# Norm statistics of a two-block kernel computed in four column groups, and the factor spread by a product

## The chip, the cores and the metric

The kernel runs on one core of one Trainium2 chip. The metric is device microseconds of one execution, from launch to the end of the program; the profile adds a trace of one execution, with the engines PE (TensorE), DVE (VectorE), ACT (ScalarE), POOL and the DMA queues.

## The reference

Two blocks in float32 over 1024 tokens of width 1024. The first is a SwiGLU layer, a mixer of latent attention and a state-space scan, a second SwiGLU layer and a gated embedding, with a layer norm (ln1 to ln4) after each. The second begins with an RMS norm (here called "h") and a modulation, and mixes by gates, convolutions and a recurrence. What the change touches are the five norms:

```
def layer_norm(x, g, b):
    mu = jnp.mean(xf, axis=-1, keepdims=True)
    var = jnp.mean(jnp.square(xf - mu), axis=-1, keepdims=True)
    y = (xf - mu) * lax.rsqrt(var + LN_EPS)
    return y * g + b

x = layer_norm(ALPHA * x + 0.5 * swiglu(x, ffn1_w1, ffn1_w3, ffn1_w2), ln1_g, ln1_b)
...                                        # mixer, then ln2
x = layer_norm(ALPHA * x + 0.5 * swiglu(x, ffn2_w1, ffn2_w3, ffn2_w2), ln3_g, ln3_b)
ple = jax.nn.sigmoid(x @ ple_w_gate) * (p @ ple_w_proj)
x = layer_norm(ALPHA * x + ple, ln4_g, ln4_b)
h = x * lax.rsqrt(jnp.mean(x * x, axis=-1, keepdims=True) + RMS_EPS) * norm_g * (1 + scale) + shift
```

## The kernel before

**Layout.** The activations lie transposed: X is 128 partitions x 8 chunks x 1024 tokens, so the 1024 features are 8 chunks k of 128 partitions. Everything runs in two halves of 512 tokens (h = 0, 1), since one PSUM bank holds 128 x 512 float32. A product of full precision is made of three passes in the replicated format fp32r: both operands are kept as a high and a low part (XS[:, 0] and XS[:, 1] for X), and `group3` issues high-high, high-low and low-high. A product over 8 chunks is so 24 matmuls of 128x512 ("a product" below), one over 2 chunks 6, over 4 chunks 12.

**A norm** takes, for each half: the sum over chunks on DVE (HELD), a float32 product of all ones with it (bank "mean": every partition gets the sum), the subtraction on DVE (8 steps "c"), the squares on ACT (8 steps, into the free high half of XS, called XSf, or into SQ), their sum, the root on ACT, the reciprocal on DVE, 8 steps "y" (X times gain times factor) on DVE, each followed by a high part on ACT and a low part on DVE, both into XS. The sum of the squares goes over partitions by a float32 product with ones into the bank "var". For ln1 h0, ln3 h0, ln4 h1 and both halves of h it is accumulated on PE over the 8 chunks (`square_sum` and the loop in `norm`); for the five pairs in SUMMED DVE adds the chunks first, and one product is left. In all 45 such products. Since ones has 128 columns, every partition of the bank holds the same 512 sums, and the root and the reciprocal run on 128 x 512.

**Order.** Every engine has its own program, written out by hand; an engine goes through it in order and waits for events of the others (`ve(...)` for DVE, `ac(...)` for ACT, `mm(...)` for PE). The steps of a norm are a generator, `norm` or `merge_norm` (or `norm_h`, for ln4 and h together); `hook()` runs it on to its next `yield`, in the middle (k = 4) or at the end of a neighbouring product. So the norm of one half lies among products of the other half or of the next layer: ln1 h0 and ln3 h0 among the last down products of their own layer ("dn", 12 matmuls each, m = 0 to 7 of h1), ln1 h1 among the products of `latents`, ln2 h1 among the first up products of the second SwiGLU layer, ln3 h1 and ln4 h0 among those of `embed` (for every n a product "pg" of 24 matmuls and a product "pp" of 6, whose sum "pe" is made on DVE), ln4 h1 and h among the first products of the mixer.

**Banks.** PSUM banks are dealt out in turn by `banks`, a ring of 7 in the first SwiGLU layer and of 8 after it. `banks.take(use, end)` names the event that ends a use; whoever comes to the same bank one round later waits for it before his first matmul. TMP, five buffers of 512 columns, is dealt out in the same way by `tmps`.

Of the kernel before, what the change touches and what calls it, by code (L numbers as in the profile page):

```python
# [252 lines left out]
def build(nc, t, plan):  # L253
# [104 lines left out]
    GW = at("GW", 188.0625, [128, 3, 128], F32)  # L358
    HX = at("HX", 184, [128, 2, 512], F32)
    VA = at("VA", 56, [128, 1030], F32)  # L360
# [118 lines left out]
    def var_bank(name, h):  # L479

        return bank(name, "var", h) if name in LNS else bank("sq", name, h)

    def out_part(p):

        return slice(0, 512) if p == 0 else slice(256 + 256 * p, 512 + 256 * p)
# [79 lines left out]
    def tensor(e):  # L565
# [23 lines left out]
        def product8(u, h, use, tag, pair=xs_pair, beside=False, within=False):  # L589
            if h == 1 and not beside:  # L590
                flush()
            e.wait_ge(w_hi(u), w_lo(u), *banks.free(use))
            for k in range(8):
                if within and k == 4:
# [12 lines left out]
        def square_sum(name, h, n, src, width=512):  # L607
# [3 lines left out]
            for k in range(n):  # L611
                e.wait_ge(ac("sq", name, h, k))
                mms([(bank(*use)[:, 0:width], ones[:], src(k), k == 0, k == n - 1)]).then_inc(*mm.inc("sq", name, h, k))

        def norm(name, h):
            mean, var = (name, "mean", h), (name, "var", h)
            banks.take(mean, (ve, name, "mean", h))
            e.wait_ge(ve("ones"), ve(name, "sum", 7, h), *banks.free(mean))
            mms([(bank(*mean), ones[:], HELD[:, h, :], True, True)]).then_inc(*mm.inc(*mean))
            banks.take(var, (ac, "rs", name, h))  # L620
            yield
            if (name, h) in SUMMED:
                yield
                e.wait_ge(ve(name, "sqs", 7, h), *banks.free(var))
                mms([(bank(*var), ones[:], squares(name, 0, h), True, True)]).then_inc(*mm.inc(name, "var", 7, h))
            else:
                e.wait_ge(*banks.free(var))
                for k in range(8):
                    if k == 4:
                        yield  # L630
                    e.wait_ge(ac(name, "sq", k, h))
                    mms([(bank(*var), ones[:], squares(name, k, h), k == 0, k == 7)]).then_inc(*mm.inc(name, "var", k, h))
            yield
            yield
            yield

        def merge_norm(h):

            mean, var = ("ln2", "mean", h), ("ln2", "var", h)
            banks.take(mean, (ve, "ln2", "mean", h))  # L640
            e.wait_ge(ve("ones"), ve("ln2", "sum", 7, h), *banks.free(mean))
            mms([(bank(*mean), ones[:], HELD[:, h, :], True, True)]).then_inc(*mm.inc(*mean))
            yield
            banks.take(var, (ac, "rs", "ln2", h))
            e.wait_ge(ve("ln2", "sqs", 7, h), *banks.free(var))
            mms([(bank(*var), ones[:], squares("ln2", 0, h), True, True)]).then_inc(*mm.inc("ln2", "var", 7, h))
            yield
# [20 lines left out]
        def ffn(name, tag, with_mod):  # L668
# [4 lines left out]
            def up(fis):  # L673

                us = {fi: (w.take(), w.take()) for fi in fis}
                for h in range(2):
                    for fi in fis:
                        use1, use3 = (name, "up1", fi, h), (name, "up3", fi, h)
                        banks.take(use1, (ac, name, "silu", fi, h))
                        banks.take(use3, (ve, name, "mul", fi, h))  # L680
                        product8(us[fi][0], h, use1, tag, within=h == 0)
# [87 lines left out]
        def latents():  # L769
            us = {i: w.take() for i in (1, 2, 0, 3, 4, 5)}  # L770
            for n, (i, h) in enumerate(LATENTS):
# [5 lines left out]
                for k in range(8):  # L777
                    if k == 4 and n in (1, 2, 3):
                        hook()
# [319 lines left out]
        def merge():  # L1099
            nonlocal side  # L1100

            def out_product(u, m, h):
                use = ("wo", m, h)
                banks.take(use, (ve, *use))
                product8(u, h, use, "mh", pair=mh_pair, beside=h == 1, within=m in (3, 6) and h == 1 or None)
            us = [w.take() for _ in range(8)]
# [10 lines left out]
        def norm_h(h):  # L1117

            steps = norm("ln4", h)
            for _ in range(3):  # L1120
                next(steps)
                yield
            square_sum("h", h, 8, lambda k: SQ[k][:])
            yield

        def embed():
# [3 lines left out]
            for n, (m, h) in enumerate(EMBED):  # L1130
# [6 lines left out]
                banks.take(use, (ac, *use))  # L1137
                product8(us[m], h, use, "ln3", beside=True, within=n in (1, 2, 3, 8, 9, 10, 12) or None)
                if h == 1 or m < 4:
# [26 lines left out]
        def first_planes():  # L1166
# [4 lines left out]
            for h in range(2):  # L1171
                if h:
                    banks.skip()
                for i, (u, (name, sig, end)) in enumerate(zip(us, names)):
# [3 lines left out]
                    for k in range(8):  # L1178
                        if k == 4 and h == 0 and i < 2:
                            next(steps)  # L1180
# [160 lines left out]
    def scalar(e):  # L1341
# [46 lines left out]
        def root(name, h, n, eps, var, end=None, width=512):  # L1388

            use = ("rs", name, h)  # L1390
            tmps.take(use, (ve, *(end or use)))
            e.wait_ge(var, ve("eps"), *tmps.free(use))
            act(tmp(*use)[:, 0:width], var_bank(name, h)[:, 0:width], ACT.Sqrt, bias=EPS[eps], scale=1.0 / n).then_inc(*ac.inc(*use))

        def norm(name, h, dead, to_xs=True):
# [7 lines left out]
            yield  # L1403
            root(name, h, 1024, LN_EPS, mm(name, "var", 7, h))
            yield
# [509 lines left out]
        def embed():  # L1915
# [50 lines left out]
            biased(0)  # L1966
            root("h", 0, 1024, RMS_EPS, mm("sq", "h", 0, 7))
            gate(12)
# [39 lines left out]
        def mixer():  # L2008
            for ct in range(4):
# [46 lines left out]
                else:  # L2056
# [7 lines left out]
                    biased(1)  # L2064
                    root("h", 1, 1024, RMS_EPS, mm("sq", "h", 1, 7))
                    for k in range(8):
# [156 lines left out]
    def vector(e):  # L2223
# [64 lines left out]
        def rstd(name, h, out, width=512):  # L2288
            e.wait_ge(ac("rs", name, h))
            d.reciprocal(out[:, 0:width], tmp("rs", name, h)[:, 0:width]).then_inc(*ve.inc("rs", name, h))  # L2290

        def norm_add(name, i, h, src, ready, held, order=range(8)):

# [8 lines left out]
        def norm(name, h, src, ready, to_xs=True):  # L2302
# [13 lines left out]
            yield  # L2316
            e.wait_ge(ve(name, "c", 7, h))
            rstd(name, h, s)
            yield
# [824 lines left out]
        def h_rows(h):  # L3144
# [5 lines left out]

            rstd("h", h, HX[:, h, :])
            for k in range(8):
                e.wait_ge(ve("gc", 1), ve("rs", "h", h), ac("ln4", "y", k, h), *tmps.free(("hp", h, k)))
                stt(tmp("hp", h, k), X[:, k, half(h)], GC[:, 0, k:k + 1], HX[:, h, :], ALU.mult, ALU.mult).then_inc(
                    *ve.inc("hy", k, h))
# [947 lines left out]
```

## Time and profile before

| what | us |
|---|---|
| median of 3 runs | 3131.28 |
| lowest and highest | 3130.58, 3132.92 |
| the profiled execution | 3131.53 |
| its span in the trace | 3129.7 |
| PE busy | 3082.8 (98%) |
| DVE busy | 2368.0 (76%) |
| ACT busy | 1222.6 (39%) |

The span runs from the first to the last instruction in the trace; 1.8 us of the execution's time lie around it. Busy time counts instructions of the engine itself. A float32 matmul stands in the trace as two records, one for each half of its weights' bits, and its PEld records (weight loads) likewise.

### The profile page before, as it was taken

Reading aid. Unit: us, or ns where it says so; the run is one execution under the profiler, and the core shown is the slowest. Engines: PE = TensorE matmul, PEld = TensorE weight load, DVE = VectorE, ACT = ScalarE, POOL = GpSimd, SP = SyncE. Lnnn points to the kernel's source line nnn. Section 1 sums busy time; section 2 is a strip of 40 time slices with the busy share of each in tenths; the row PEclk is TensorE's granted clock in tenths of the full one; section 3 lists DMA queues with packets and bytes.
Section 4 is the critical chain, followed back from the end, with each engine's and each line's share of the span. In section 5 each row is a group of like instructions: output and inputs, shape, how many; then the busy total and the mean of one; then the engine's idle time right before and its main releaser. Section 6 shows DMA issues by size and latency. Waiting matters only on the chain.

```text
span 3129.7 us, 37552 instructions
## 1 busy us (share of the span) xinstructions
PE 3082.8 (98%) x14712; PEld 2490.4 (80%) x14712; DVE 2368.0 (76%) x4017; ACT 1222.6 (39%) x1884; POOL 56.2 (2%) x49
## 2 busy tenths in 40 slices
PE   8999999999999999999999999999999999999998
PEld 6887888877988887777878888888777788788887
DVE  6777767778869678888598776767797789789736
ACT  4233323335342455554243233222366534534414
POOL 0000000000000001130000000000000000000000
PEclk9999999999999999999999999999999999999999
DMA  3222212223343351012212111111211221122242
GB/s 131 74 73 75 81 61 68 68 68 109 119 101 135 115 197 56 8 48 114 95 54 68 41 54 61 48 54 48 68 54 63 104 77 64 48 70 101 81 168 74
DMA packets 89247, 250.13 MB, mean 80 GB/s; under 512 B 8560, under 2 KB 24816, under 8 KB 87536
## 3 DMA queue, kind: packets, MB, share of 16 engines
q1 hardware_dynamic: 89072, 247.73, 23.5%
q8 instruction: 118, 1.93, 0.3%
q14 instruction: 57, 0.47, 0.0%
HBM read 203.65 MB, written 44.04 MB: 79 GB/s over the span
## 4 chain that ended last, share of the span: by engine, by line
PE 90%; DVE 7%; ACT 2%; issue 1%; DMA 0%; DVEq 0%; SPq 0%; ACTq 0%
PE PS L577 88%; PE PS L582 2%; DVE WS L2228 1%; DVE X L2236 1%; DVE XS L2236 1%; DVE HELD L2290 1%; DVE X L2228 1%; ACT XS L1345 0%; DVE COLB L3038 0%; DVE XSf L2228 0%; ACT XSf L1345 0%; DVE TMP L2228 0%; DMA RAW<-in_W 0%; DVE TMP L2232 0%; ACT WS L1345 0%
## 5 line engine op out<-in xcount | busy, mean ns | idle before, releaser
L577 PE MATMUL PS<-XS,WS 128*128 128x512 f32 (+1 forms) x6480 | 1513.8, 391 | 20.4 <-DVE XS L2228 9.5
L577 PEld LDWEIGHTS PS<-XS,WS 128*128 128x128 f32 x6480 | 1208.9, 188 | 297.8 <-issue 27.1
L577 PE MATMUL PS<-HS,WS 128*128 128x512 f32 x2208 | 511.0, 390 | 3.1 <-DVE TMP L2228 2.7
L577 PEld LDWEIGHTS PS<-HS,WS 128*128 128x128 f32 x2208 | 414.1, 188 | 93.1 <-DVE TMP L2228 3.5
L2228 DVE TENSOR_TENSOR WS<-RAW,WS 128x512 fp32r<-128x512 f32 (+1 forms) x398 | 346.9, 880 | 173.8 <-ACT WS L1345 173.2
L1345 ACT ACTIVATE WS<-RAW 128x512 fp32r<-128x512 f32 (+1 forms) x398 | 307.6, 779 | 398.7 <-PE PS L577 344.0
L2228 DVE TENSOR_TENSOR X<-PS,X 128x512 f32<-128x512 f32 x272 | 184.2, 688 | 101.8 <-PE PS L577 101.7
L2228 DVE TENSOR_TENSOR TMP<-TMP,PS 128x512 f32<-128x512 f32 x304 | 203.6, 682 | 61.5 <-PE PS L577 58.7
L577 PE MATMUL PS<-T,WS 128*128 128x512 f32 x960 | 230.6, 389 | 0.0
L577 PEld LDWEIGHTS PS<-T,WS 128*128 128x128 f32 x960 | 180.2, 188 | 37.4
L1345 ACT ACTIVATE TMP<-PS 128x512 f32<-128x512 f32 x144 | 85.0, 596 | 291.0 <-PE PS L577 274.4
L2236 DVE SCALAR_TENSOR_TENSOR CV<-UU,COL,CV 128x1024 f32<-128x1024 f32 x120 | 154.0, 1283 | 3.4
L1345 ACT ACTIVATE HS<-TMP 128x512 fp32r<-128x512 f32 x88 | 55.6, 632 | 211.3 <-DVE TMP L2236 197.2
L577 PE MATMUL PS<-T1h_ln,WS 128*128 128x512 f32 x320 | 105.0, 389 | 0.0
L577 PE MATMUL PS<-KH,QH 128*128 128x512 f32 x384 | 104.0, 406 | 0.0
L1345 ACT ACTIVATE TMP<-TMP 128x512 f32<-128x512 f32 x80 | 50.6, 632 | 101.3 <-DVE TMP L2228 101.3
L2228 DVE TENSOR_TENSOR HS<-TMP,HS 128x512 fp32r<-128x512 f32 x88 | 60.6, 689 | 32.3 <-ACT HS L1345 32.1
L3038 DVE TENSOR_REDUCE COLB<-PS 128x1 f32<-128x1024 f32 x64 | 77.9, 1218 | 5.7 <-PE PS L577 4.6
L577 PE MATMUL PS<-MH,WS 128*128 128x512 f32 x256 | 80.3, 393 | 0.0
L1345 ACT ACT_TABLE_LOAD x56 | 71.8, 1283 | 15.1 <-DVE GG L2228 10.7
L1345 ACT ACTIVATE WS<-RAWX 128x512 fp32r<-128x512 f32 x66 | 41.4, 627 | 91.2 <-PE PS L577 91.1
L577 PEld LDWEIGHTS PS<-KH,QH 128*128 128x128 f32 x384 | 67.5, 189 | 11.3
(338 smaller groups left out, 3580.6 us busy)
## 6 DMA issues: line engine op xcount, KB each, us to landing
RAW<-in_W SPq DMA_DIRECT2D x263, 512.0 KB, 3.3
RAWX<-in_W SPq DMA_DIRECT2D x30, 512.0 KB, 3.3
DC<-TMP SPq DMA_DIRECT2D x32, 256.0 KB, 2.1
X<-in_xT SPq DMA_DIRECT2D x8, 512.0 KB, 8.9
DX<-X SPq DMA_DIRECT2D x2, 2048.0 KB, 8.4
DCZ<-CA SPq DMA_DIRECT2D x8, 512.0 KB, 4.1
DGA<-TMP SPq DMA_DIRECT2D x16, 256.0 KB, 2.3
DGB<-TMP SPq DMA_DIRECT2D x16, 256.0 KB, 3.1
```

The lines of the kernel that those rows point to most:

```text
L577: done = d.matmul(out, l, r, start=first, stop=last)
L582: done = d.transpose(out, x, idn)
L1345: return d.activation(out, x, f, bias=bias, scale=scale)
L2228: return d.tensor_tensor(out, a, b, op)
L2236: return d.scalar_tensor_tensor(out=out, in0=a, scalar=s, in1=b, op0=op0, op1=op1)
L2290: d.reciprocal(out[:, 0:width], tmp("rs", name, h)[:, 0:width]).then_inc(*ve.inc("rs", name, h))
L3038: d.tensor_reduce(mx, PS[:, 2 + 2 * (n % 2):4 + 2 * (n % 2), :], AX.XY, ALU.max).then_inc(*ve.inc("mx", n))
```

## The change

Five things change, and the SUMMED list and all other sums of squares (kv, q, cx, c, out) stay.

1. **Sum of squares.** `quarter_sums` replaces each of the 45 products by four, each with 32 columns of ones and 128 tokens: quarter g of the half goes to partitions 32g to 32g+31 of the bank, columns 0 to 127.
2. **Root and reciprocal** run on 128 x 128; the reciprocal is written in place, into TMP, and HX is dropped.
3. **`spread`** is new: four float32 products of 128x128, whose weights are column 32g of the identity, repeated 128 times. They put row 32g of the reciprocal on all partitions, into columns 128g to 128g+127 of the same bank. It waits for the reciprocal. It happens ten times, once for each norm and half.
4. **The steps y** (and "hy", for h) take the factor from that PSUM bank instead of HELD or HX, and wait for the spread.
5. **The bank "var"** (and "sq" for h) is freed by the last of the eight steps y, before by the root. Extra hooks at k = 7 give the spread its place, 9 matmuls after the sum where both are in one product.

```
+        def quarter_sums(out, src, first, last):
+            return mms([(out[32 * g:32 * g + 32, 0:128], ones[:, 0:32], src[:, 128 * g:128 * g + 128], first, last)
+                        for g in range(4)])
+        def spread(name, h):
+            r = tmp("rs", name, h)
+            e.wait_ge(ve("rs", name, h), dma("const")("cols"))
+            mms([(var_bank(name, h)[:, 128 * g:128 * g + 128], ident[:, 32 * g:32 * g + 1].to_broadcast([128, 128]), r[:, 0:128], True, True)
+                 for g in range(4)]).then_inc(*mm.inc("rb", name, h))
...
         def norm(name, h):
-            banks.take(var, (ac, "rs", name, h))
+            banks.take(var, (ve, name, last_scaled(name), 7, h))
             yield
             if (name, h) in SUMMED:
                 yield
                 e.wait_ge(ve(name, "sqs", 7, h), *banks.free(var))
-                mms([(bank(*var), ones[:], squares(name, 0, h), True, True)]).then_inc(*mm.inc(name, "var", 7, h))
+                quarter_sums(bank(*var), squares(name, 0, h), True, True).then_inc(*mm.inc(name, "var", 7, h))
...
-            yield
-            yield
+            yield
+            spread(name, h)
             yield
...
-                product8(us[m], h, use, "ln3", beside=True, within=n in (1, 2, 3, 8, 9, 10, 12) or None)
+                product8(us[m], h, use, "ln3", beside=True,
+                         within={1: (4,), 2: (4,), 3: (4, 7), 8: (4,), 9: (4,), 10: (4, 7), 12: (4, 7)}.get(n))
...
+        def rstd_rows(name, h):
+            r = tmp("rs", name, h)[:, 0:128]
+            e.wait_ge(ac("rs", name, h))
+            d.reciprocal(r, r).then_inc(*ve.inc("rs", name, h))
...
-                e.wait_ge(ve("rs", name, h), ac(name, "sq", 7, h))
-                scaled = stt(x, x, col(name + "_g", k), s, ALU.mult, ALU.mult)
+                e.wait_ge(mm("rb", name, h), ac(name, "sq", 7, h), ve(name, "c", 7, h))
+                scaled = stt(x, x, col(name + "_g", k), var_bank(name, h), ALU.mult, ALU.mult)
```

PE around the sum of squares of ln3 h1, in `embed`, before. XSf holds the squares, XS the activations of the products pg, HS (with WS) those of the products pp; the x23 and x5 rows end a product each:

```order
2729 L577 MATMUL PS<-XSf,ones 128x512 [waits vector_done]
2730 L577 MATMUL PS<-XS,WS 128x512 x12
2731 L577 MATMUL PS<-HS,WS 128x512 [waits vector_done]
2732 L577 MATMUL PS<-HS,WS 128x512 x5
2733 L577 MATMUL PS<-XS,WS 128x512 [waits activation_done,weight_lo_done,weight_hi_done]
2734 L577 MATMUL PS<-XS,WS 128x512 x23
2735 L577 MATMUL PS<-HS,WS 128x512 [waits weight_lo_done,weight_hi_done]
2736 L577 MATMUL PS<-HS,WS 128x512 x5
2737 L577 MATMUL PS<-XS,WS 128x512 [waits activation_done]
```

The same place after. TMP holds the reciprocal:

```order
2767 L579 MATMUL PS<-XSf,ones 32x128 [waits vector_done]
2768 L579 MATMUL PS<-XSf,ones 32x128 x3
2769 L579 MATMUL PS<-XS,WS 128x512 x9
2770 L579 MATMUL PS<-TMP,ident 128x128 [waits vector_done]
2771 L579 MATMUL PS<-TMP,ident 128x128 x3
2772 L579 MATMUL PS<-XS,WS 128x512 x3
2773 L579 MATMUL PS<-HS,WS 128x512 x6
2774 L579 MATMUL PS<-XS,WS 128x512 [waits activation_done,weight_lo_done,weight_hi_done]
2775 L579 MATMUL PS<-XS,WS 128x512 x23
2776 L579 MATMUL PS<-HS,WS 128x512 [waits weight_lo_done,weight_hi_done]
2777 L579 MATMUL PS<-HS,WS 128x512 x5
2778 L579 MATMUL PS<-XS,WS 128x512 [waits vector_done]
```

Row 2770, the spread, is new and waits for the reciprocal. Row 2778 is the first matmul of pg(5, 0), which comes to the bank of the sum one round of 8 later: before it waited for ACT's root (row 2737), now for DVE's last step y.

PE at the last down products of the first SwiGLU layer (ln1 h0), from the second run of sums on, before; the last product is dn m = 7, which comes to the bank of the sum in a ring of 7:

```order
797 L577 MATMUL PS<-XSf,ones 128x512 [waits activation_done] x4
798 L577 MATMUL PS<-HS,WS 128x512 x24
799 L577 MATMUL PS<-HS,WS 128x512 [waits vector_done]
800 L577 MATMUL PS<-HS,WS 128x512 x11
801 L577 MATMUL PS<-HS,WS 128x512 [waits vector_done]
802 L577 MATMUL PS<-HS,WS 128x512 x11
803 L577 MATMUL PS<-HS,WS 128x512 [waits activation_done]
804 L577 MATMUL PS<-HS,WS 128x512 x11
```

Rows 798 to 804 are dn m = 3 to 7. The same place on PE after, from the last sum on:

```order
810 L579 MATMUL PS<-XSf,ones 32x128 [waits activation_done]
811 L579 MATMUL PS<-XSf,ones 32x128 x3
812 L579 MATMUL PS<-HS,WS 128x512 x12
813 L579 MATMUL PS<-TMP,ident 128x128 [waits vector_done]
814 L579 MATMUL PS<-TMP,ident 128x128 x3
815 L579 MATMUL PS<-HS,WS 128x512 x36
816 L579 MATMUL PS<-HS,WS 128x512 [waits vector_done]
817 L579 MATMUL PS<-HS,WS 128x512 x11
```

The spread stands after m = 3 (row 813), and m = 7 (row 816) waits for the last step y of ln1 h0. On DVE and ACT no instruction changes its place; root, reciprocal and the eight steps y stand where they stood.

## Rows read from the trace of the kernel before

**Rows 1.** The page, busy time of each engine.

```profile
PE 3082.8 (98%) x14712; PEld 2490.4 (80%) x14712; DVE 2368.0 (76%) x4017; ACT 1222.6 (39%) x1884; POOL 56.2 (2%) x49
```

**Rows 2.** PE by time, eight sums of squares of h h0: start, us, count.

```profile
2360.96 7.03 PE L577 MATMUL PS<-SQ,ones 128*128 128x512 f32 x16
2367.42 3.30 PE L577 MATMUL PS<-XS,WS 128*128 128x512 f32 x12
2370.56 1.52 PE L577 MATMUL PS<-HS,WS 128*128 128x512 f32 x6
```

**Rows 3.** PE by time, products in two column groups of 64, then full ones.

```profile
906.83 1.97 PE L577 MATMUL PS<-UB,BW 128*64 128x128 f32 x32
908.73 1.09 PE L582 MATMUL PS<-ident,BT 128*128 128x128 f32 x8
909.75 1.97 PE L577 MATMUL PS<-UB,BW 128*64 128x128 f32 x32
```

**Rows 4.** Groups by form, DVE: count, busy us, mean ns.

```profile
L2290 DVE RECIPROCAL HELD<-TMP 128x512 f32<-128x512 f32 x11 | 36.9, 3350 | 17.1 <-ACT TMP L1345 17.1
L2290 DVE RECIPROCAL HELD<-TMP 128x256 f32<-128x256 f32 x3 | 5.2, 1750 | 1.2 <-ACT TMP L1345 1.2
L2236 DVE SCALAR_TENSOR_TENSOR X<-PS,MOD,X 128x512 f32<-128x512 f32 x40 | 29.7, 747 | 46.6 <-PE PS L577 41.4 <-DMA X<-DX 5.2
```

**Rows 5.** By time, ln1 h0: DVE around its reciprocal, PE at its end.

```profile
699.91 3.35 DVE L2290 RECIPROCAL HELD<-TMP 128x512 f32<-128x512 f32 x1 [1.93 <-ACT TMP L1345]
704.45 1.41 DVE L2236 SCALAR_TENSOR_TENSOR X<-X,COL,HELD 128x512 f32<-128x512 f32 x2
716.47 0.75 DVE L2236 SCALAR_TENSOR_TENSOR X<-X,COL,HELD 128x512 f32<-128x512 f32 x1
...
712.60 3.71 PE L577 MATMUL PS<-XS,WS 128*128 128x512 f32 x15
```

**Rows 6.** By time, ln3 h1: PE, then DVE, then ACT.

```profile
2295.62 1.02 PE L577 MATMUL PS<-XSf,ones 128*128 128x512 f32 x2
2306.05 1.52 PE L577 MATMUL PS<-HS,WS 128*128 128x512 f32 x6
2307.41 5.60 PE L577 MATMUL PS<-XS,WS 128*128 128x512 f32 x24
2331.95 1.02 PE L577 MATMUL PS<-HELD,ones 128*128 128x512 f32 x2
...
2300.79 3.34 DVE L2290 RECIPROCAL HELD<-TMP 128x512 f32<-128x512 f32 x1
2305.13 1.40 DVE L2236 SCALAR_TENSOR_TENSOR X<-X,COL,HELD 128x512 f32<-128x512 f32 x2
2319.96 0.75 DVE L2236 SCALAR_TENSOR_TENSOR X<-X,COL,HELD 128x512 f32<-128x512 f32 x1
...
2300.86 1.06 ACT L1345 ACTIVATE WS<-RAW 128x1024 fp32r<-128x1024 f32 x1 [3.50 <-PE PS L577]
```

**Rows 7.** By time, ln4 and h of h0: DVE, then ACT.

```profile
2349.57 3.34 DVE L2290 RECIPROCAL HELD<-TMP 128x512 f32<-128x512 f32 x1
...
2367.34 1.28 ACT L1345 ACT_TABLE_LOAD   x1
```

**Rows 8.** By time, ln4 and h of h1: PE, then DVE.

```profile
2410.58 11.46 PE L577 MATMUL PS<-XS,WS 128*128 128x512 f32 x48
...
2443.45 23.60 PE L577 MATMUL PS<-XS,WS 128*128 128x512 f32 x102 [0.40 <-ACT XS L1345]
...
2429.67 3.35 DVE L2290 RECIPROCAL HX<-TMP 128x512 f32<-128x512 f32 x1 [8.92 <-ACT TMP L1345]
```

**Rows 9.** Three stretches: us; PE, PEld, DVE, ACT, POOL busy; granted clock.

```profile
712.00:753.00 41.00, 36.16 (x145) 26.20 (x144) 36.09 (x50) 22.11 (x35) 0.00 (x0) 0.99 0.33 117
749.00:752.40 3.40, 1.73 (x7) 0.84 (x6) 3.27 (x6) 2.11 (x3) 0.00 (x0) 1.00 0.31 115
752.40:755.80 3.40, 3.40 (x8) 2.49 (x9) 2.99 (x9) 2.24 (x4) 0.00 (x0) 0.50 0.00 0
```

More of the change, by code:

```diff
@@ L358, in build @@
     GW = at("GW", 188.0625, [128, 3, 128], F32)
-    HX = at("HX", 184, [128, 2, 512], F32)
     VA = at("VA", 56, [128, 1030], F32)
@@ L481, in var_bank, with last_scaled @@
         return bank(name, "var", h) if name in LNS else bank("sq", name, h)
+    def last_scaled(name):
+        return "y0" if name == "ln4" else "y"
     def out_part(p):
@@ L593, in product8 @@
             for k in range(8):
-                if within and k == 4:
+                if within and k in within:
                     hook()
@@ L631, in norm @@
                     e.wait_ge(ac(name, "sq", k, h))
-                    mms([(bank(*var), ones[:], squares(name, k, h), k == 0, k == 7)]).then_inc(*mm.inc(name, "var", k, h))
+                    quarter_sums(bank(*var), squares(name, k, h), k == 0, k == 7).then_inc(*mm.inc(name, "var", k, h))
             yield
-            yield
+            spread(name, h)
             yield
@@ L643, in merge_norm @@
             yield
-            banks.take(var, (ac, "rs", "ln2", h))
+            banks.take(var, (ve, "ln2", "y", 7, h))
             e.wait_ge(ve("ln2", "sqs", 7, h), *banks.free(var))
-            mms([(bank(*var), ones[:], squares("ln2", 0, h), True, True)]).then_inc(*mm.inc("ln2", "var", 7, h))
+            quarter_sums(bank(*var), squares("ln2", 0, h), True, True).then_inc(*mm.inc("ln2", "var", 7, h))
+            yield
+            spread("ln2", h)
             yield
@@ L680, in up @@
                         banks.take(use3, (ve, name, "mul", fi, h))
-                        product8(us[fi][0], h, use1, tag, within=h == 0)
+                        product8(us[fi][0], h, use1, tag, within=None if h else (4, 7) if fi else (4,))
                         product8(us[fi][1], h, use3, tag, within=None if h == 0 else False)
@@ L777, in latents @@
                 for k in range(8):
-                    if k == 4 and n in (1, 2, 3):
+                    if k == 4 and n in (1, 2, 3) or k == 7 and n == 3:
                         hook()
@@ L1104, in out_product @@
                 banks.take(use, (ve, *use))
-                product8(u, h, use, "mh", pair=mh_pair, beside=h == 1, within=m in (3, 6) and h == 1 or None)
+                product8(u, h, use, "mh", pair=mh_pair, beside=h == 1, within={3: (4,), 6: (4, 7)}.get(m) if h else None)
             us = [w.take() for _ in range(8)]
@@ L1119, in norm_h @@
             steps = norm("ln4", h)
-            for _ in range(3):
+            for _ in range(4):
                 next(steps)
                 yield
-            square_sum("h", h, 8, lambda k: SQ[k][:])
+            use = ("sq", "h", h)
+            banks.take(use, (ve, "hy", 7, h))
+            e.wait_ge(*banks.free(use))
+            for k in range(8):
+                e.wait_ge(ac("sq", "h", h, k))
+                quarter_sums(bank(*use), SQ[k], k == 0, k == 7).then_inc(*mm.inc("sq", "h", h, k))
+            yield
+            spread("h", h)
             yield
@@ L1178, in first_planes @@
                     for k in range(8):
-                        if k == 4 and h == 0 and i < 2:
+                        if k == 4 and h == 0 and i in (0, 1, 2, 4):
                             next(steps)
@@ L1390, in root @@
             use = ("rs", name, h)
-            tmps.take(use, (ve, *(end or use)))
+            tmps.take(use, (mm, "rb", name, h) if width == 128 else (ve, *(end or use)))
             e.wait_ge(var, ve("eps"), *tmps.free(use))
@@ L1403, in norm @@
             yield
-            root(name, h, 1024, LN_EPS, mm(name, "var", 7, h))
+            root(name, h, 1024, LN_EPS, mm(name, "var", 7, h), width=128)
             yield
@@ L1966, in embed @@
             biased(0)
-            root("h", 0, 1024, RMS_EPS, mm("sq", "h", 0, 7))
+            root("h", 0, 1024, RMS_EPS, mm("sq", "h", 0, 7), width=128)
             gate(12)
@@ L2064, in mixer @@
                     biased(1)
-                    root("h", 1, 1024, RMS_EPS, mm("sq", "h", 1, 7))
+                    root("h", 1, 1024, RMS_EPS, mm("sq", "h", 1, 7), width=128)
                     for k in range(8):
@@ L2316, in norm @@
             yield
-            e.wait_ge(ve(name, "c", 7, h))
-            rstd(name, h, s)
+            rstd_rows(name, h)
             yield
@@ L3149, in part @@
                     ALU.add, ALU.subtract).then_inc(*ve.inc("xs", "h", k, h))
-            rstd("h", h, HX[:, h, :])
+            rstd_rows("h", h)
             for k in range(8):
-                e.wait_ge(ve("gc", 1), ve("rs", "h", h), ac("ln4", "y", k, h), *tmps.free(("hp", h, k)))
-                stt(tmp("hp", h, k), X[:, k, half(h)], GC[:, 0, k:k + 1], HX[:, h, :], ALU.mult, ALU.mult).then_inc(
+                e.wait_ge(ve("gc", 1), mm("rb", "h", h), ac("ln4", "y", k, h), *tmps.free(("hp", h, k)))
+                stt(tmp("hp", h, k), X[:, k, half(h)], GC[:, 0, k:k + 1], var_bank("h", h), ALU.mult, ALU.mult).then_inc(
                     *ve.inc("hy", k, h))
```

## The prediction, made before the changed kernel ran

> **What bounds the kernel now.** The page comes first: PE is busy for 3082.8 of 3129.7 us [rows 1]. Where PE is never idle, a change is worth what it takes from PE's own work. So the next view is PE by time around each norm, with DVE and ACT beside it: which of them is late when PE comes to a product that needs the norm. The last are the groups by form, for the price of one instruction.
>
> A product of 128x512 costs 0.227 us in a row (2306.05 to 2307.41 for six) [rows 6]. Eight float32 sums of squares cost 2370.56 - 2360.96 - 12 x 0.227 = 6.88 us, 0.86 each [rows 2]; the busy time of such a row overlaps its neighbour's, so I go by starts.
>
> **The sums in column groups.** The nearest case is UB,BW, whose products write 64 of the 128 columns. Let p be one record over 128 tokens, s the cost of a change of shape. The full ones: 8p + s = 909.75 - 908.73 = 1.02. The halves: 32 records in 908.73 - 906.83 = 1.90, and if two run side by side 16p + s = 1.90 [rows 3]. That gives p = 0.11 and s = 0.14, and 0.11 is what 128 tokens in a two-record product should take if 512 take 0.43. Two groups do run side by side. No row shows four. Bounds: four side by side, 2p = 0.22 a product; pairs only, 0.44; nothing side by side, 0.88, as much as now. I take 0.22, since the step from one group to two cost nothing, and two changes of shape (0.28) for every run. The 45 products are six runs of four, two of eight and five single ones: 38.7 us before, 9.9 + 13 x 0.28 = 13.5 after. A single one costs 0.5, a run of four 1.2, one of eight 2.0.
>
> The row shows loads of the second group going on beside the first group's products. The Trainium skill says otherwise ("TensorE: Matmul & The Clock Gate", Part 3, The mechanism): weight loads overlap with running products only where the row group differs, and these share it. By that rule four groups run one after the other, and the sums cost 4.5 us more than now; by the row they cost 25 us less.
>
> **The spread** is eight full records, 8p = 0.88 to 1.02 with a change [rows 3]; I take 0.95, ten times 9.5. **On PE alone** the change is 13.5 + 9.5 - 38.7 = -15.7 us.
>
> **DVE.** A reciprocal takes 3350 ns on 512 columns and 1750 on 256 [rows 4], 6.25 ns a column; on 128 some 950 (bounds 150 and 1750, the line is the nearest). That is 2.4 us less, ten times. The steps y read the factor from PSUM; a step with a PSUM source takes 747 ns [rows 4], one from SBUF 0.75 us [rows 5]: nothing. The root gets shorter too; no term rests on it.
>
> **Where it lies.** What counts is the path, and two waits are new on PE, which works in order: the spread waits for the reciprocal, and the bank of the sum is held until the eighth step y, so that whoever comes one round later waits for that.
>
> *ln1.* DVE is free at 697.98 (699.91 less 1.93) [rows 5]; the sums end by then, and the reciprocal runs to 698.95, PE spreads until 699.9, and y begins at 700.1 against 704.45. All behind it on DVE moves by 4.35, and the last y (716.47 + 0.75) ends at 712.87. dn m = 7, in a ring of seven, can't begin before; PE would be there at 708.0 (699.9 and 36 products): a wait of 4.9 us. It ends at 715.6, 3.0 later than before (712.60). Then XS is all there, and the stretch 712 to 753, with 4.8 us idle on PE [rows 9], takes 4.1 less: 3.2 for waits on XS that fall away, 0.9 for h1, whose shorter root lets ACT go on to XS earlier. Sum -1.1.
>
> *ln2.* Single sums: 0.36 saved, 0.95 for the spread, and at h1 1.3 of waiting for a reciprocal, which shorter waits on XS give back: +0.6 and -0.2, together +0.4.
>
> *ln3 h0* repeats ln1 h0 with a ring of eight; the wait moves to the first product of `embed`, which waited for XS anyway: -0.2, bounds -1 and +2.
>
> *ln3 h1* is the largest term. The sum starts at 2295.6, nine products on, at 2298.2, PE comes to the spread. The reciprocal starts at 2300.79 without having waited for anything but DVE's queue [rows 6], ends at 2301.7: PE waits 3.6. Spread to 2302.7, nine products to 2304.7. ACT's copy of a weight at 2300.86 had waited 3.50 for that same end of pp(3, 0) [rows 6], and now goes at 2304.9; with its 1.06 and DVE's low half (1.0, the time between reciprocal and first y) y starts at 2307.1, 2.0 later than 2305.13 although the reciprocal was shorter. The last y ended 15.6 after the first: now 2322.7. PE has done 30 more products by 2311.5 and stands before pg(5, 0) for 11.2 us. It starts 15.3 later than 2307.41; up to the mean at 2331.95 there are 24.5 us with 102 products (23.1), so 1.4 of slack comes back: +13.9. If DVE moved 2.4 earlier instead of 2.0 later, it would be +9.5; with ACT's copy later by another 2, +16.
>
> *ln4 and h, h0.* The reciprocal at 2349.57 hangs on DVE's queue [rows 7] and ends at 2350.5; PE is there 1.5 earlier. The eight sums of h then take 2.0 instead of 6.9, but ACT loads its table for the root at 2367.34 without a wait [rows 7]: its queue sets it, not the sums, and shifts by 1.1 with PE's lateness. Root and reciprocal end at 2371.1, PE waits 4.0, and is through with pg(0, 1) at 2372.7 against 2370.56: +2.1.
>
> *ln4 and h, h1* gains. Two runs save 4.6: 2411.0 becomes 2406.4. 12 products, spread, 36 products, eight sums, 12 products and spread give 2424.1; the factor before was there at 2429.67 + 3.37 = 2433.0 [rows 8]. PE waits for XS up to 2443.45 [rows 8], so all 8.9 count: -8.9.
>
> Sum: -1.1 + 0.4 - 0.2 + 13.9 + 2.1 - 8.9 = +6.2.
>
> **The clock.** From 749.0 to 752.4 PE was busy for 1.73 of 3.40 us, and in the next 3.4 us the granted clock was 0.50 (1.2 GHz instead of 2.4) and PE did 8 products where 15 fit [rows 9]: 1.6 us. In four of the new waits (4.9, 3.6, 11.2, 4.0) PE idles longer than the 1.7 us of that stretch. I count three falls: +4.8, bounds 0 and 10. Span 3129.7 + 6.2 + 4.8 = 3140.7; with the 1.8 us around it 3142.5, and the median of the runs lies 0.25 under the profiled execution: 3142.
>
> **Rivals.** (1) *The clock stays up*, as over the lighter idling of rows 8: 3137.5. (2) *Groups don't run side by side*, a product's weights waiting for the product before: 0.88 each. The runs of ln4 and h in h1 cost 10.4 more, ln1 h0 and ln3 h0 some 1.6 each as the sum becomes late for DVE, single ones 0.6: 3158; pairs only, 3147. The skill's rule would give the first. (3) *Faster:* the wait of pg(5, 0) for its bank is the one place that decides. If the last y of ln3 h1 comes before PE gets there, at 2311.5, the 13.9 shrink to the 2.4 of the spread's wait, and with one fall of the clock less the time is 3129; below 3125 if the other spreads find their reciprocal ready. That needs 8.6 us from the reciprocal to the last y where the trace has 19.9 [rows 6], with two weights and the sum pe of pp(3, 0) between. Against it also: before, the bank was needed 13.3 us ahead of that y.
>
> **Numbers.** Forecast with two to five falls 0.62 (3139 to 3148); rival 1 0.14; pairs only 0.08; none side by side 0.04; faster or near it 0.12. Range 3133 to 3151. A measurement can tell 0.2% (6.3 us) from no change. Slower by more takes the forecast, both cases of (2) and half of (1): 0.81; within, half of (1) and half of (3): 0.13; faster 0.06.
>
> **What would show it.** XSf and SQ sums at 32x128 with four starts a few ns apart and a run of four in 1.2 us; reciprocals near 0.95; PE idle about 11 us before pg(5, 0), 5 before dn m = 7, 4 before the spread of h h0, released by DVE; granted clock 0.5 after them; the stretch from h1's mean of ln4 to the mixer 9 us shorter; PE's own work 15 us less. It is wrong if PE doesn't idle at pg(5, 0), or if the sums take as long as now.

## The result, and the profile after

| what | before | after |
|---|---|---|
| median of 4 runs each, us | 3132.1 | 3146.97 |
| lowest and highest | 3130.58, 3132.93 | 3145.39, 3150.2 |
| the profiled execution's span | 3129.7 | 3146.6 |
| granted clock, mean over the span | 0.998 | 0.993 |

The changed kernel is slower by 0.49% (ratio 1.0049, 95% interval 1.0034 to 1.0065), 14.9 us by the medians and 16.9 us by the spans. The forecast was 3142 and its range 3133 to 3151.

The page of the changed kernel, busy time of each engine (it answers to [rows 1]), and from its list of groups the two kinds of products that wait most, with what ended most of their waiting:

```profile
PE 3075.7 (98%) x15062; PEld 2498.8 (79%) x15062; DVE 2345.7 (75%) x4017; ACT 1220.1 (39%) x1884; POOL 56.2 (2%) x49
...
L579 PE MATMUL PS<-XS,WS 128*128 128x512 f32 (+1 forms) x6480 | 1512.7, 391 | 28.1 <-DVE X L2260 13.2
...
L579 PE MATMUL PS<-HS,WS 128*128 128x512 f32 x2208 | 516.2, 393 | 7.8 <-DVE X L2260 4.6
```

PE, DVE and ACT all have less to do than before. But PE waits, and 13.2 + 4.6 us of that are ended by one line of DVE, L2260, the helper that issues the steps y among others. So the view to open next is PE by time where those waits lie. The largest is at ln3 h1 (it answers to [rows 6]):

```profile
2296.57 0.43 PE L579 MATMUL PS<-XSf,ones 128*32 128x128 f32 x8
2296.93 2.34 PE L579 MATMUL PS<-XS,WS 128*128 128x512 f32 x9
2302.66 2.08 PE L579 MATMUL PS<-TMP,ident 128*128 128x128 f32 x8 [3.39 <-DVE TMP L2320]
2304.39 1.63 PE L579 MATMUL PS<-XS,WS 128*128 128x512 f32 x3
2305.81 2.75 PE L579 MATMUL PS<-HS,WS 128*128 128x512 f32 x6
2308.37 5.67 PE L579 MATMUL PS<-XS,WS 128*128 128x512 f32 x24
2313.88 1.52 PE L579 MATMUL PS<-HS,WS 128*128 128x512 f32 x6
2326.50 8.43 PE L579 MATMUL PS<-XS,WS 128*128 128x512 f32 x24 [11.09 <-DVE X L2260]
```

The sum is four side-by-side quarters, 0.36 us from its start to the next product's. Nine products on, PE waits 3.39 us for the reciprocal, and the spread takes twice what it takes elsewhere. Then pg(5, 0) waits 11.09 us for the bank. DVE and ACT in the same stretch show why it is 11:

```profile
2301.66 0.94 DVE L2320 RECIPROCAL TMP<-TMP 128x128 f32<-128x128 f32 x1
2309.75 1.23 DVE L2252 TENSOR_TENSOR WS<-RAW,WS 128x1024 fp32r<-128x1024 f32 x1 [7.15 <-ACT WS L1369]
2310.89 1.40 DVE L2260 SCALAR_TENSOR_TENSOR X<-X,COL,PS 128x512 f32<-128x512 f32 x2
...
2325.70 0.74 DVE L2260 SCALAR_TENSOR_TENSOR X<-X,COL,PS 128x512 f32<-128x512 f32 x1
```

```profile
2308.66 1.06 ACT L1369 ACTIVATE WS<-RAW 128x1024 fp32r<-128x1024 f32 x1 [11.22 <-PE PS L579]
```

The reciprocal is done at 2302.6, and the first y starts at 2310.89, because DVE's low half of a weight stands before it, that waits for ACT's copy at 2308.66, and that for the end of PE's product pp(3, 0). The eighth y ends at 2326.44; pg(5, 0) starts at 2326.50.

The clock, in windows of the changed kernel (start and end, length, the busy times of PE, PEld, DVE, ACT and POOL with their counts, the granted clock, DMA share and GB/s):

```profile
2302.70:2308.40 5.70, 5.70 (x18) 4.83 (x19) 0.00 (x0) 0.00 (x0) 0.00 (x0) 0.50 0.00 0
...
2326.50:2332.30 5.80, 5.80 (x14) 4.54 (x15) 4.55 (x7) 1.19 (x2) 0.00 (x0) 0.50 0.00 0
...
2391.80:2397.20 5.40, 5.40 (x17) 4.63 (x18) 1.41 (x2) 2.27 (x4) 0.00 (x0) 0.50 0.00 0
```

After the waits of 3.4, 11.1 and 3.8 us PE worked for 5.4 to 5.8 us at 1.2 GHz, and after that of 4.6 us before dn m = 7 for 3.4 us. Before, there was one such stretch near a norm, of 3.4 us [rows 9].

The other places. dn m = 7 at the end of ln1 h0, which answers to [rows 5], and the eight sums and the spread of h h0, which answer to [rows 2]:

```profile
701.27 8.44 PE L579 MATMUL PS<-HS,WS 128*128 128x512 f32 x36
714.35 4.62 PE L579 MATMUL PS<-HS,WS 128*128 128x512 f32 x12 [4.64 <-DVE X L2260]
...
2383.76 1.95 PE L579 MATMUL PS<-SQ,ones 128*32 128x128 f32 x64
2385.65 2.33 PE L579 MATMUL PS<-XS,WS 128*128 128x512 f32 x9
2391.79 2.08 PE L579 MATMUL PS<-TMP,ident 128*128 128x128 f32 x8 [3.81 <-DVE TMP L2320]
```

And where the change gains, from the mean of ln4 h1 to the last wait for XS of h h1 (it answers to [rows 8]):

```profile
2420.52 1.02 PE L579 MATMUL PS<-HELD,ones 128*128 128x512 f32 x2
...
2443.95 1.96 PE L579 MATMUL PS<-SQ,ones 128*32 128x128 f32 x64
...
2460.14 0.93 PE L579 MATMUL PS<-XS,WS 128*128 128x512 f32 x3 [0.39 <-ACT XS L1369]
```

39.6 us; before, the mean started at 2395.04 and the last wait ended at 2443.45, 48.4 us.

**The ledger.** PE's instructions other than those of the norms are the same in both kernels, so the start of each can be compared. "Lateness" is how much later such an instruction starts in the changed kernel than in the one before, in us:

| stretch | lateness at its end | gained or lost in it | forecast, without the clock |
|---|---|---|---|
| start to ln1 | +1.5 | +1.5 | 0 |
| ln1 | +1.2 | -0.3 | -1.1 |
| ln2 and mixer | +0.9 | -0.2 | +0.4 |
| ln3 h0 | +1.0 | 0.0 | -0.2 |
| ln3 h1 | +20.5 | +19.5 | +13.9 |
| ln4 and h, h0 | +25.5 | +5.0 | +2.1 |
| ln4 and h, h1 | +16.7 | -8.8 | -8.9 |

One norm of ten makes more than the whole loss. What is left in dispute is why: the bank that is held, the new wait for the reciprocal, the clock, or the column groups.

### The profile page after: what moved, and what is told of

Its sections match the earlier page's. It is cut to its first block, busy times and chain, and to the rows that moved or that the text cites. A ratio compares the mean times of both kernels' runs of the same rounds, so it can differ in the third digit from the quotient of the medians.

```text
span 3146.6 us, 38237 instructions
## 1 busy us (share of the span) xinstructions
PE 3075.7 (98%) x15062; PEld 2498.8 (79%) x15062; DVE 2345.7 (75%) x4017; ACT 1220.1 (39%) x1884; POOL 56.2 (2%) x49
## 4 chain that ended last, share of the span: by engine, by line
PE 90%; DVE 7%; ACT 2%; issue 1%; DMA 0%; DVEq 0%; SPq 0%; ACTq 0%
PE PS L579 88%; PE PS L584 2%; DVE X L2252 1%; DVE WS L2252 1%; DVE X L2260 1%; DVE XS L2260 1%; ACT WS L1369 0%; ACT XSf L1369 0%; DVE COLB L3067 0%; DVE XSf L2252 0%; DVE TMP L2252 0%; ACT XS L1369 0%; ACT X L1369 0%; DVE HELD L2252 0%; DMA RAW<-in_W 0%
## 5 line engine op out<-in xcount | busy, mean ns | idle before, releaser
L579 PE MATMUL PS<-XS,WS 128*128 128x512 f32 (+1 forms) x6480 | 1512.7, 391 | 28.1 <-DVE X L2260 13.2
L2260 DVE SCALAR_TENSOR_TENSOR CV<-UU,COL,CV 128x1024 f32<-128x1024 f32 x120 | 154.1, 1284 | 3.4
L579 PEld LDWEIGHTS PS<-KH,QH 128*128 128x128 f32 x384 | 67.5, 189 | 11.2
```

The costliest lines, as they stand in the source:

```text
L579: done = d.matmul(out, l, r, start=first, stop=last)
L2260: return d.scalar_tensor_tensor(out=out, in0=a, scalar=s, in1=b, op0=op0, op1=op1)
```

## The experiments

The kernels below are made from the changed one by sets of norms, (name, h), at the top; without them they are instruction for instruction the changed kernel, or with an empty QUARTER the one before:

```
+QUARTER = all ten        # column groups, root and reciprocal on 128 columns, spread
+HOLD = QUARTER           # the bank of the sum is freed by the last step y
+COPY = SKIP = SWAP = LATER = none
+    def var_end(name, h):
+        if (name, h) in COPY:
+            return (ve, "fc", name, h)
+        if (name, h) in HOLD:
+            return (ve, "hy", 7, h) if name == "h" else (ve, name, last_scaled(name), 7, h)
+        return (ac, "rs", name, h)
...
-            banks.take(var, (ve, name, last_scaled(name), 7, h))
+            banks.take(var, var_end(name, h))
```

Each was timed in turns with the kernel before on the same chip; its median there was 3131.5 or 3131.6 us. The changed kernel itself was timed only with the result above (3146.97, where the kernel before had 3132.1), and its four runs lie 4.8 us apart, so a small difference to it says little.

### One bank left out: pg(5, 0)

```
+SKIP = {("ln3", 1)}
...
+                if n == 0 and ("ln3", 0) in SKIP or n == 5 and ("ln3", 1) in SKIP:
+                    banks.skip()
                 banks.take(use, (ac, *use))
```

> The changed kernel, but pg(5, 0) leaves out the bank that holds the factor of ln3 h1 and takes the next one of the ring (and all behind it move on by one). My theory is that the held bank causes the 11.1 us of idle before pg(5, 0) and the half clock after it. Then pg(5, 0) starts right after pp(4, 0), at about 2315.4 instead of 2326.5, at full clock (5.6 us for its 24 matmuls instead of 8.3); 1.5 us of slack that the late start had used come back as a wait. 3147 - 11.1 - 2.9 + 1.5 = 3134.5, bounds 3131 and 3138. The rival is that something else is late there (the squares, the activations of h1, a weight): the idle time then stays before pg(5, 0) or one product later, and the time stays above 3142.

Measured: 3133.9 us (ratio 1.0007, 0.9998 to 1.0016). PE by time at the same place:

```profile
2307.90 5.71 PE L591 MATMUL PS<-XS,WS 128*128 128x512 f32 x24
2313.45 1.52 PE L591 MATMUL PS<-HS,WS 128*128 128x512 f32 x6
2314.82 5.60 PE L591 MATMUL PS<-XS,WS 128*128 128x512 f32 x24
2320.26 1.52 PE L591 MATMUL PS<-HS,WS 128*128 128x512 f32 x6
```

pg(5, 0) now starts at 2314.82, right behind pp(4, 0), at full clock; nothing waits in its place. Another bank for this product gives back 13 of the 14.9 us. The half clock after the 3.4 us wait for the reciprocal is still there.

### The hold alone, on the kernel before

```
+QUARTER = none
+HOLD = all ten
```

> The kernel before with one thing of the change: the bank of the sum of squares of all ten norms is freed by the last step y and no longer by the root. Sums, root, reciprocal and steps y stay as they were; there is no spread. My theory is that holding the bank is what costs: in ln3 h1 the last y ended at 2320.7 where pg(5, 0) began at 2307.4, so +13.3, less 1.4 of slack, and 3 of half clock; in ln1 h0 the last y ended at 717.2 where PE comes to dn m = 7 at 709.9, so 7.3 and 2.7 of half clock, of which some 6 come back from the waits on XS; ln3 h0 +2. Together 3132 + 15 + 4 + 2 = 3153, bounds 3146 and 3159. The rival is that the spread and its waits are the cost and the hold is covered: then 3132 to 3135.

Measured: 3158.46 us (1.0084, 1.007 to 1.0097), 26.9 us slower, without a single one of the other edits. PE by time where it waits:

```profile
717.30 5.00 PE L591 MATMUL PS<-HS,WS 128*128 128x512 f32 x12 [7.23 <-DVE X L2282]
...
2281.55 2.04 PE L591 MATMUL PS<-XS,WS 128*128 128x512 f32 x4 [4.71 <-DVE X L2282]
...
2332.39 7.47 PE L591 MATMUL PS<-XS,WS 128*128 128x512 f32 x24 [13.20 <-DVE X L2282]
```

The waits of 7.2 and 13.2 us are those that were worked out; the one of pg(0, 0), 4.7, was taken as 2, and less of the first came back (lateness 9.5 after dn m = 7, still 6.5 at the end of ln1). That makes most of the 5 us over the estimate. The rival falls. The hold costs the old kernel more than a copy saves the changed one (20 us, below); its wait before dn m = 7 is 7.2 us against 4.6, since the changed kernel's shorter sums, root and reciprocal bring y forward there.

### The gain alone: ln4 h1 and h h1

```
+QUARTER = {("ln4", 1), ("h", 1)}
```

> The kernel before with the whole change, but for ln4 h1 and h h1 alone (24 of the 45 sums, two spreads). My theory is that the stretch from the mean of ln4 h1 to the mixer is where the change pays: it was 48.4 us before and 39.6 after, so 3132 - 8.8 = 3123, bounds 3121 and 3126. The rival is that this gain came from the late start of that stretch (DVE and ACT had 20 us more to run ahead of PE): then PE waits for XS as before and the time is 3128 to 3132.

Measured: 3123.52 us (0.9971, 0.996 to 0.9983). PE comes to this stretch within 1 us of the kernel before and is 8.05 us ahead behind it. The gain is the change's own and doesn't hang on the 25 us by which PE came late to it.

### The width of the column groups

```
-            return mms([(out[32 * g:32 * g + 32, 0:128], ones[:, 0:32], src[:, 128 * g:128 * g + 128], first, last)
+            return mms([(out[:, 0:128], ones[:], src[:, 128 * g:128 * g + 128], first and g == 0, last and g == 3)
                         for g in range(4)])
```

> The changed kernel, but the four products of a sum have all 128 columns of ones and the same target, so that they can't run side by side and each occupies the whole array (all four are added up into the same 128 columns, so the factor is not the right one; only the time counts). If the four column groups ran side by side in the changed kernel, a sum now takes 0.88 us instead of some 0.25: 45 x 0.63 = 28 us of PE work more, of which 10 lie in ln4 h1 and h h1, where nothing covers them, and about 7 more on the paths of the two h0 norms of the SwiGLU layers and the single sums; the rest goes into waits that are there anyway. 3147 + 18 = 3165, bounds 3158 and 3172. If the groups ran one after the other there too, nothing changes: 3147.

Measured: 3164.51 us (1.0105, 1.0091 to 1.0119). The run of four sums in ln4 h1, PE by time, here and then in the changed kernel (for each the sums and the product after them; the difference of the starts is the cost):

```profile
2431.48 3.73 PE L597 MATMUL PS<-SQ,ones 128*128 128x128 f32 x32
2434.97 2.98 PE L597 MATMUL PS<-XS,WS 128*128 128x512 f32 x12
```

```profile
2426.95 1.08 PE L579 MATMUL PS<-SQ,ones 128*32 128x128 f32 x32
2427.97 3.01 PE L579 MATMUL PS<-XS,WS 128*128 128x512 f32 x12
```

3.49 against 1.02 us for the same 32 records over the same tokens. At full width a sum costs 0.87 us, as much as one product of 128x512 had cost [rows 2]; in four column groups 0.25. The edit also gives the four products one target. That is not what costs: the four products of a spread, full width too, go to four ranges of columns, and their 8 records take 0.81 us (2434.77 to 2435.58), 0.10 each, where 3.49 us for 32 is 0.11.

The first 30 ns of the same two runs, instructions on SQ alone (length, then busy time and count of PE, PEld, DVE, ACT), first in the changed kernel and then at full width:

```profile
2426.95:2426.98 0.03, 0.03 (x4) 0.03 (x4) 0.00 (x0) 0.03 (x1) 1.00 0.00 0
```

```profile
2431.48:2431.51 0.03, 0.03 (x1) 0.03 (x1) 0.00 (x0) 0.03 (x1) 1.00 0.00 0
```

Four products and four weight loads against one of each. So the quarters do run side by side, and this is worth 17.5 us to the changed kernel. The Trainium skill's rule ("TensorE: Matmul & The Clock Gate", Part 3, The mechanism), that weight loads overlap with running products only where the row group differs, is not what this case shows: all four share their rows. That the groups would then run one after the other was the prediction's own inference from that rule, not a statement of the page.

### A copy of the factor

```
+COPY = QUARTER
...
+            if (name, h) in COPY:
+                e.wait_ge(mm("rb", name, h))
+                d.tensor_copy(kept, var_bank(name, h)).then_inc(*ve.inc("fc", name, h))
+                return kept, ve("fc", name, h)
```

`kept` is HELD, or HX for h, as in the kernel before.

> The changed kernel, but DVE copies the factor from its bank into SBUF right after the spread (one instruction of 128x512, 0.7 us, ten times) and frees the bank with that; the steps y read the copy. By the theory of the held banks the waits before dn m = 7, pg(0, 0) and pg(5, 0) go (with their half clock), as they did when those three left the bank out (3129.4), and the wait of 4.9 us at 1177 which came with the shifted ring doesn't come, with 2 of half clock. Against it stand 0.7 us later activations in ln1, ln3 h0, ln4 h1 and h h1, where PE waits for them: +3. 3129.4 - 5 + 3 = 3127.5, bounds 3124 and 3131. The rival is that DVE's ten copies push back more than they free: above 3134.

Measured: 3127.13 us (0.9982, 0.9973 to 0.9991), with four single runs from 3122.24 to 3122.83 and seven from 3127.07 to 3128.49. The trace is of the fastest, so its lateness (-9.3 us at the end) holds for the four. By form, DVE:

```profile
L2348 DVE COPY HELD<-PS 128x512 f32<-128x512 f32 x8 | 5.5, 690 | 6.7 <-PE PS L591 6.7
...
L2348 DVE COPY HX<-PS 128x512 f32<-128x512 f32 x2 | 1.4, 691 | 2.5 <-PE PS L591 2.5
```

Seven us of DVE work take away the waits for a bank before dn m = 7, pg(0, 0) and pg(5, 0): by the medians 20 us less than the changed kernel. With all ten norms changed it is 0.2% faster than the kernel before. The trace also prices the clock: at ln3 h1 PE waits as long for the reciprocal as in the changed kernel, but in this execution the clock stays up.

```profile
2293.17 1.16 PE L591 MATMUL PS<-TMP,ident 128*128 128x128 f32 x8 [3.41 <-DVE TMP L2342]
...
2296.23 5.60 PE L591 MATMUL PS<-XS,WS 128*128 128x512 f32 x24
```

Spread and nine products take 3.06 us from start to start, in the changed kernel 5.71 (2302.66 to 2308.37): 2.65 us for that fall alone.

### Three banks left out

```
+SKIP = {("ln1", 0), ("ln3", 0), ("ln3", 1)}
```

> The changed kernel, but dn m = 7 of the first SwiGLU layer, pg(0, 0) and pg(5, 0) each leave out the bank that holds a factor (ln1 h0, ln3 h0, ln3 h1) and take the next one. By the theory that the held banks cause all three waits: as for ln3 h1 alone, 3134.5, less what dn m = 7 gains. It starts 4.6 us earlier and at full clock, which brings the down products of h1, and with them the norm of ln1 h1, 5 us forward (bounds 0 and 6.5), and pg(0, 0) 1 (bounds 0 and 2): 3128.5, bounds 3125 and 3134. The rival for these two is that the activations XS come at the same time whichever bank is used: then the same time as for ln3 h1 alone.

Measured: 3129.35 us (0.9994, 0.9985 to 1.0002), 4.6 below the kernel with one bank left out: the activations didn't come at the same time regardless. PE is 5.8 us ahead of the kernel before at the end of ln1. It loses that later, in the mixer:

```profile
1181.99 2.47 PE L591 MATMUL PS<-CKV,WS 128*128 128x512 f32 x5 [4.88 <-DVE TMP L2274]
```

The kernel with the copies comes there 6 us ahead too and doesn't wait. Leaving a bank out moves all later uses on by one, so that every later use has another predecessor; that points to the ring, but was not tried alone.

### The spread of h h0 later

```
-                         within={1: (4,), 2: (4,), 3: (4, 7), 8: (4,), 9: (4,), 10: (4, 7), 12: (4, 7)}.get(n))
+                         within={1: (4,), 2: (4,), 3: (4, 7), 8: (4,), 9: (4,), 10: (4, 7), 12: (4,), 13: (7,)}.get(n))
```

> The changed kernel, but the spread of h h0 stands in the product after the next, 30 matmuls (6.8 us) later. Its wait of 3.8 us for the reciprocal, which hangs on ACT's queue, is then covered, and the 6.8 us of half clock behind it (3.4 us of work) don't come, if the clock fell because PE idled there: 3147 - 3.8 - 3.4 = 3140, bounds 3137 and 3142. If the clock falls whatever stands there, 3143.5. The rival is that the factor was needed then, so that the steps y 3 us later give a wait for XS or for the bank: 3147.

Measured: 3144.9 us (1.0044, 1.003 to 1.0057), between the forecast (bounds up to 3142) and the rival, so neither came. The 2.1 us to the changed kernel are less than the spread of its four runs; the traces give 2.2. PE by time, at the spread and at the mean of ln4 h1:

```profile
2394.04 1.05 PE L597 MATMUL PS<-TMP,ident 128*128 128x128 f32 x8
...
2416.76 2.07 PE L597 MATMUL PS<-HELD,ones 128*128 128x512 f32 x2 [3.26 <-DVE HELD L2284]
```

The spread waits for nothing and takes 1.05 us, not 2.08. Behind it PE is 7.2 us ahead of the changed kernel. It was 0.6 ahead before this place, so 6.6 are due to the edit: the 3.8 of the wait and 2.7 for the 5.4 us of work at half clock (forecast 3.8 and 3.4). Without the idle stretch the clock didn't fall here, in this one trace. Then 5.0 of the 7.2 go again. DVE goes through the steps y and the last sums for the mean of ln4 h1 at its own pace:

```profile
2416.01 0.69 DVE L2284 TENSOR_TENSOR HELD<-HELD,X 128x512 f32<-128x512 f32 x1
```

```profile
2418.07 0.69 DVE L2252 TENSOR_TENSOR TMP<-TMP,PS 128x512 f32<-128x512 f32 x1 [2.72 <-PE PS L579]
2418.79 0.69 DVE L2252 TENSOR_TENSOR X<-X,TMP 128x512 f32<-128x512 f32 x1
2419.52 0.69 DVE L2252 TENSOR_TENSOR HELD<-HELD,X 128x512 f32<-128x512 f32 x1
```

The first row is the last addition before the mean here, the last row that of the changed kernel. There DVE waited 2.72 us for PE; here PE, 7 us further, waits 3.26 for DVE, and with the wait the half clock comes back. The rival had the direction, that most of it returns as a wait, but the wait is for the sum of ln4 h1, which neither reading had named.

### Nine of ten norms

```
+QUARTER = all ten without ("ln3", 1)
```

> The changed kernel with one of its ten norms put back: ln3 h1 sums, takes root and reciprocal and frees its bank as in the kernel before. By the starts on PE this norm alone cost 19.6 us (lateness of 1.1 at the mean of ln3 h1, 20.6 at that of ln4 h0): 3147 - 19.6 = 3127.4, bounds 3124 and 3131, which is faster than the kernel before. The rival is that the lateness only gathers there, and DVE, ACT or the other held banks would bring half of it in later (ln4 h0, h h0): 3132 to 3140.

Measured: 3129.08 us (0.9992, 0.9983 to 1.0001; single runs from 3125.71 to 3130.28), 17.9 us less than the whole change, and no different from the kernel before. The lateness doesn't gather there, it arises there.

### The norms that pay

```
+QUARTER = {("ln1", 0), ("ln1", 1), ("ln3", 0), ("ln4", 1), ("h", 0), ("h", 1)}
+SKIP = {("ln3", 0)}
+SWAP = {("ln1", 0)}
+LATER = {("ln3", 0)}     # its spread one yield later
... within: 12: (4,), 13: (7,)
```

> The change for ln1 (both halves), ln3 h0, ln4 h1 and both halves of h; ln2, ln3 h1 and ln4 h0 as in the kernel before. dn m = 7 swaps its bank with its follower in the ring, pg(0, 0) leaves the held bank out, the spread of ln3 h0 stands one product of 12 later (it had waited 2.0) and that of h h0 30 matmuls later (it had waited 3.8). By my ledger of PE starts: ln1 -6.2, and no 4.9 us of idle at 1177 since the ring keeps its phase; ln3 h0 -2.5 to -4.5; h h0 -3.6 (eight sums 6.9 to 2.0, spread 0.95, changes of shape); ln4 h1 and h h1 -8.6. Together 3132 - 22 = 3110, bounds 3106 and 3119. The rival is that DVE and ACT set the time once PE is 10 us ahead of where it was, and the gains of ln1 and ln3 come back as waits: 3119 to 3123.

Measured: 3117.84 us (0.9957, 0.9945 to 0.997). That is inside the bounds, but 8 us over the estimate and close to the rival's 3119. PE by time, the two waits that took most of the difference:

```profile
713.75 2.55 PE L597 MATMUL PS<-XS,WS 128*128 128x512 f32 x10 [2.11 <-DVE X L2292]
...
2387.70 1.12 PE L597 MATMUL PS<-HELD,ones 128*128 128x512 f32 x2 [3.27 <-DVE HELD L2284]
```

The first is the swapped bank itself: its next user now comes before the last y. The second is the late sum of ln4 h1 again. Whether DVE as a whole was the bound or these two places, the next kernel tells.

```
+COPY = {("ln1", 0), ("ln3", 0)}
+SKIP = SWAP = none
... within: 12: (4,), 13: (4,)
```

> As the kernel with the chosen norms (ln1, ln3 h0, ln4 h1 and h changed; ln2, ln3 h1 and ln4 h0 as before), which took 3117.8, with two places mended. There the first product of XS waited 2.1 us for the swapped bank, until the last step y of ln1 h0: now DVE copies the factor of ln1 h0 and of ln3 h0 into SBUF and frees the bank, and the ring is dealt out as it is (-2.1, +0.7 for the copy where PE waits for XS of ln1 h1). And the spread of h h0 stood 2.0 us behind its reciprocal, which made DVE late for the sum of ln4 h1, where PE idled 3.3 us and had 3.4 us of half clock: now it stands 9 matmuls earlier (-2.0, and -1.7 if the clock stays up). 3117.8 - 1.4 - 3.7 = 3112.7, bounds 3110 and 3117. The rival is that DVE's queue as a whole and not the spread makes the sum of ln4 h1 late: then the 3.3 us of idle stay and the time is 3116 or 3117.

Measured: 3113.03 us (0.9941, 0.9928 to 0.9953). PE by time at the same two places:

```profile
711.12 8.32 PE L597 MATMUL PS<-XS,WS 128*128 128x512 f32 x36
...
2385.28 1.13 PE L597 MATMUL PS<-HELD,ones 128*128 128x512 f32 x2 [1.23 <-DVE HELD L2284]
```

It was the two places, for all but the 1.2 us of wait that the second still has. This kernel is 18.5 us (0.59%) faster than the one before and 34 us faster than the whole change, with the same idea in it.

## Why the prediction held, and where it was off

- **The sign and the mechanism** were right. The cost is the bank held to the last y in ln3 h1; experiments with one bank left out, with the hold alone, with a copy and with that norm put back each give 13 to 27 us.
- **Column groups**: four side by side, as chosen between the bounds. Runs of four took 1.0 us (forecast 1.2), of eight 1.9 (2.0), single ones 0.36 (0.5), a spread 0.81 to 0.91 at full clock (0.95).
- **PE's own work**: forecast 15 less. The busy time is 7.1 less, but PE worked 27 us at half clock where before it was 7, which adds some 10: 17 less.
- **Reciprocal and y**: ten reciprocals at 949 ns (950), a step y from PSUM 742 ns where it had been 745 from SBUF (nothing).
- **Waits**: 4.6 before dn m = 7 (4.9), 3.4 at the spread of ln3 h1 (3.6), 11.1 before pg(5, 0) (11.2), 3.8 at the spread of h h0 (4.0).
- **ln4 and h, h1**: -8.8 (-8.9).
- **The mis-sized term is the clock.** +4.8 was made of three falls of 1.6, from one fall in the trace of before, and it came to about +10, at the upper bound of 10. All four long new waits brought a fall, and behind three of them PE worked for 5.4 to 5.8 us at half clock, which costs 2.7 to 2.9 each. With 10 in place of 4.8 the forecast's sum is 16 us, and the spans differ by 16.9: the 5 us between forecast and result are this term. At ln3 h1 the spread and nine products behind it took 5.7 us instead of 3.0. These 2.7 (2.65 against the kernel with copies) are passed on: ACT's weight copy hangs on the end of those products, DVE's low half on it, the first y on that (2310.89 where 2307.1 was forecast, 1.0 of the difference being lateness from before), the bank on the last y. A further 2.9 came after pg(5, 0), 2.7 after the spread of h h0. With them 13.9 becomes 19.5 (measured 19.5) and 2.1 becomes 4.8 (5.0). That the 11.1 were forecast right hid this: PE itself came 3.9 later to the wait (2315.4, forecast 2311.5). How many falls come, and how long they last, is luck as far as these runs show (last section); the range held because its bound left 5 us for it.
- **ln1** gained 0.8 less than forecast. The half clock after dn m = 7 costs 1.7, and the one of the kernel before at 752.4 [rows 9], 1.6, no longer comes; the two cancel. What is left is that of the later waits on XS 3.4 us came back where 4.1 were forecast.
- **Not foreseen**: two falls behind waits of 2 us that both kernels have, at 69 and 1134 us, +1.5 and +1.6; one that only the kernel before had, at 1452, takes 1.7 off again. The first lies ahead of every changed instruction; the other two follow waits for which no run shows a tie to the change.

## What to carry to other kernels

When a result moves from SBUF to PSUM, its bank's lifetime grows from one read to the last: find who gets that bank next round and what he would be waiting for, before counting what the instructions save. Here the same edit was worth -18.5 or +14.9 us, depending on banks freed by a 0.7 us copy, on where the spread stands, and on which norms have it. And an idle PE costs its wait plus the slower work behind it, which can delay the very engine it will wait for next.

## What the runs showed of the hardware

- Four column groups of 32, one set of 128 rows, float32: 0.25 us a sum, against 0.87 at full width. Width in columns is what separated them, not the number of instructions (32 records in both rows), nor the one target (a spread has four and costs as much a record).
- The same wait doesn't always bring the same clock. PE idles 2.01 us for DVE before a product at about 68 us in the kernel before, in the changed one, in the one with copies and in the one with chosen norms; the clock then fell for 3.4 us in the second and fourth and stayed at 1.00 in the first and third:

```profile
64.00:80.00 16.00, 13.91 (x60) 11.21 (x61) 15.97 (x27) 7.74 (x14) 0.00 (x0) 1.00 0.31 99
```

```profile
64.00:80.00 16.00, 13.99 (x55) 11.08 (x54) 15.96 (x27) 7.12 (x12) 0.00 (x0) 0.89 0.31 99
```

  These are the same 16 us in the kernel with copies and in that with the chosen norms. Three or four such places, 1.6 us each, would fit the spread of several us between executions of one kernel; no run shows it. The long waits vary too. After the same 3.4 us before the spread of ln3 h1 PE worked at half clock for 5.8 us in the changed kernel and in the one with one bank left out, for 3.4 us in those with three banks left out and with the later spread of h h0, and not at all in the one with copies. After all other idle stretches of 3.3 us and more in these traces PE worked at half clock for 2.9 to 6.1 us. What decides, in the short waits and in the long ones, was not tried.
